# A GLA and stick-breaking decoder step: the attention mask moved into the scan, parts stored by pair and span, stores issued by ScalarE

## The reference, cut to what matters

```
proj = rmsnorm(x) @ w                     # q, k, v, gate rows
z = q . k / 8 + bias[head]                # every query t, key s
lneg = where(s < t, log_sigmoid(-z), 0)
suffix = reverse_cumsum(lneg) - lneg      # sum over s < j < t
w = where(s < t, exp(log_sigmoid(z) + suffix), 0)
o = w @ v                                 # strictly causal: s < t only
```

## Time and profile before

| | us |
|---|---|
| median of 3 runs | 3365.58 (3365.28 to 3365.92) |
| profiled execution, its own time | 3368.11 |
| its span | 3366.5 |
| mean granted TensorE clock | 0.969 of 2.4 GHz |
| PE busy | 3155.3 (94%) |
| DVE busy | 1661.5 (49%) |
| ACT busy | 1399.5 (42%) |
| POOL busy | 889.0 (26%) |

### The profile page before, as it was taken

The page is one execution under the profiler, slowest core; times in us unless marked ns, Lnnn a source line. Parts: engine busy times, 40 slices in busy tenths (PEclk is TensorE's granted clock), DMA queues, the critical chain, the costliest instruction groups (busy, mean ns, idle before and its releaser), DMA issues. The chain is left out here.

```text
span 3366.5 us, 49760 instructions
## 1 busy us (share of the span) xinstructions
PE 3155.3 (94%) x17836; PEld 2474.9 (74%) x17836; DVE 1661.5 (49%) x1967; ACT 1399.5 (42%) x2332; POOL 889.0 (26%) x936
## 2 busy tenths in 40 slices
PE   6999999799799799999999499999999999799998
PEld 6999999556588699999999355555555555466665
DVE  5111122387544411222222388998899897443442
ACT  5111111265311211112211278888888787344442
POOL 0000000254111000000000266776677675100000
PEclk8999999799899899999999699999999999899999
DMA  4122111455255421444431555343433410999995
GB/s 152 62 71 76 69 57 58 159 187 182 103 183 178 147 76 51 176 170 147 165 101 57 137 151 142 79 123 107 119 88 103 123 36 16 354 325 374 366 339 210
DMA packets 257393, 489.74 MB, mean 145 GB/s; under 512 B 27133, under 2 KB 142562, under 8 KB 245922
## 3 DMA queue, kind: packets, MB, share of 16 engines
q1 hardware_dynamic: 232450, 350.61, 32.3%
q0 software_dynamic: 24752, 136.63, 11.3%
HBM read 329.58 MB, written 157.59 MB: 145 GB/s over the span
## 5 line engine op out<-in xcount | busy, mean ns | idle before, releaser
L1736 POOL TENSOR_TENSOR att_w<-att_w,att_rest 128x1023 f32<-128x1023 f32 (+7 forms) x384 | 615.4, 1606 | 303.0 <-DVE att_rest L1703 289.9
L470 PE MATMUL projb_acc<-projb_x_hi,projb_w_hi 128*128 128x416 f32 x1280 | 451.0, 352 | 16.5 <-DVE projb_w_lo L452 16.5
L470 PE MATMUL projb_acc<-projb_x_hi,projb_w_lo 128*128 128x416 f32 x1280 | 449.2, 351 | 0.0
L470 PE MATMUL projb_acc<-projb_x_lo,projb_w_hi 128*128 128x416 f32 x1280 | 448.9, 351 | 0.0
L1564 PEld LDWEIGHTS att_wT_acc<-const_ident,att_w 128*128 128x128 f32 x2176 | 236.9, 142 | 210.2 <-issue 152.9
L1653 ACT ACTIVATE att_rest<-att_z,att_bias 128x1024 f32<-128x1024 f32 (+7 forms) x384 | 333.3, 868 | 85.4 <-PE att_z L1610 55.5
L1703 DVE TENSOR_TENSOR_SCAN att_rest<-att_rest,att_zero 128x128 f32<-128x128 f32 (+7 forms) x256 | 355.0, 1402 | 23.2 <-ACT att_rest L1653 23.1
L292 PE MATMUL proja_acc<-proja_x_hi,proja_w_hi 128*128 128x416 f32 x1000 | 353.7, 354 | 0.8 <-DVE proja_x_lo L265 0.7
L292 PE MATMUL proja_acc<-proja_x_hi,proja_w_lo 128*128 128x416 f32 x1000 | 351.8, 352 | 0.0
L292 PE MATMUL proja_acc<-proja_x_lo,proja_w_hi 128*128 128x416 f32 x1000 | 350.0, 350 | 0.0
L1564 PE MATMUL att_wT_acc<-const_ident,att_w 128*128 128x128 f32 x2176 | 314.9, 281 | 31.2 <-ACT att_k_tok L1668 14.8
(11 more groups left out here) (256 smaller groups left out, 4910.4 us busy)
## 6 DMA issues: line engine op xcount, KB each, us to landing
smp_k_pages<-in_cache_k SPq DMA_DIRECT2D x128, 512.0 KB, 7.2
smp_v_pages<-in_cache_v SPq DMA_DIRECT2D x128, 512.0 KB, 7.2
proj_b<-projb_out POOLq DMA_DIRECT2D x32, 1040.0 KB, 4.4
proj_a<-proja_out POOLq DMA_DIRECT2D x24, 1040.0 KB, 4.5
kq_hi<-early_area POOLq DMA_DIRECT2D x16, 1024.0 KB, 6.0
kq_lo<-early_area POOLq DMA_DIRECT2D x16, 1024.0 KB, 8.9
att_q_hi<-kq_hi SPq DMA_DIRECT2D x60, 256.0 KB, 4.1
att_q_lo<-kq_lo SPq DMA_DIRECT2D x60, 256.0 KB, 5.1
```

The costliest lines, as they stand in the source:

```text
L470: mm = pe.matmul(acc[:, q, 0:size], w[:, b, k, :], x[:, k, at:at + size], start=(k == 0 and w is w_hi and x is x_hi), stop=(k == KD - 1 an ...
L1736: pool.tensor_tensor(these, these, passed[:, 1:size], ALU.mult).then_inc(w_made, 1)
```

## The change

- The masking matmul goes. `begin` is an identity, transposed into the last 128 columns of a PSUM bank in bfloat16 with zeros before them; the scan of a step that is not carried reads it backwards as data1 and starts from 0, so the running product is 0 until the diagonal adds its 1. Carried steps broadcast its first zero. GpSimd's multiply takes one column more.
- The parts go to DRAM as `k_parts` and `q_parts`, by pair, span, part: ACT issues four stores of half of the partitions for a block (2 KB runs) in place of two of all. A pair's keys come back in one load (L1461 to L1468 before), a span's queries in four as before, each row now 4 KB in one run. The first pieces of pair 0 are no longer cut at the first tile.
- ACT issues the stores of both projections and waits for them at the end; GpSimd has no work there.
- The turns of pair 0 move to beats 6, 8, 10, 12; the first value step of a group waits for its own turn, not for all.
- GLA's gate weights of the second head are asked for ahead of the six output weights. ACT loads the sqrt table at the head of the first and third stage.

```diff
 normalise_project, scalar:
+            act.preload_act_table_set("sqrt_and_others")
             act.wait_ge(eps_set, 1)
...
+                if gate:
+                    act.wait_ge(gate_made, (n - first_gate) * n_spans + n_spans)
+                else:
+                    act.wait_ge(copied, n * n_spans + n_spans)
+                act.wait_ge(gain_in, 32)
+                act.dma_start(dst[ds(n * P, width), :], out[0:width, b, :]).then_inc(stored[b], 16)
 project, scalar (the gpsimd blocks of both are deleted):
                         if q == 0 and from_tile(no, 1):
-                            act.wait_ge(parts_stored, no * 32)
+                            act.wait_ge(parts_stored, no * 64)
...
+                act.dma_start(dst[ds(jb * P + row, P), :], out[:, b, :]).then_inc(stored[b], 16)
+                if kind == "parts":
+                    act.wait_ge(high_made, no * n_spans + n_spans)
+                    act.wait_ge(low_made, no * n_spans + n_spans)
+                    to = parts[j].rearrange("a u e p h n -> e h p (a u) n")
+                    for part, made in enumerate((high, low)):
+                        for h in range(2):
+                            act.dma_start(to[part, h, :, ds(jb * NCH, NCH), :],
+                                          made(0, SEQ).bitcast(F32)[h * HD:(h + 1) * HD, :].rearrange("p (u n) -> p u n", n=BANK)
+                                          ).then_inc(parts_stored, 16)
 gla, sync:
-            early.load(sp)
             sp.wait_ge(logit_cp, 5)
             gate_weights(1)
+            early.load(sp)
 out_project, scalar:
+            act.preload_act_table_set("sqrt_and_others")
 attention_schedule:
-            put(7 + m if pair == 0 else 40 * (pair - 1) + LAG + 1 + 2 * m, ("turn", pair, m))
+            put(6 + 2 * m if pair == 0 else 40 * (pair - 1) + LAG + 1 + 2 * m, ("turn", pair, m))
 prompt_attention, sync:
             def load_k(pair):
-                for u in range(NCH):
-                    load_k_span(pair, u, 0, 4, in_k[pair % 2])
+                sp.dma_start(k2[:, pair % 2, :, :, :], k_parts[pair].rearrange("u e p h n -> (e p) u (h n)")
+                             ).then_inc(in_k[pair % 2], 16)
+            def load_first_k(u):
+                sp.dma_start(k2[:, 0, u, :, :], k_parts[0, u].rearrange("e p h n -> (e p) (h n)")).then_inc(in_first_k[u], 16)
             def load_q(pair, g):
                 for part, dst in enumerate((q_hi, q_lo)):
                     for half in range(2):
-                        sp.dma_start(dst[half * HD:(half + 1) * HD, g, :, :],
-                                     head_rows(part, q_parts + pair * P)[:, :, g * BANK:(g + 1) * BANK]
-                                     ).then_inc(in_q[g], 16)
+                        sp.dma_start(dst[half * HD:(half + 1) * HD, g, :, :], q_parts[pair, g, part]).then_inc(in_q[g], 16)
...
-            load_first_q(0, 0, 1)
-            load_first_k(0, 0, 1)
+            load_q(0, 0)
+            load_first_k(0)
             sp.dma_start(bias[:, 0, :], b_sb.unsqueeze(0).broadcast_to([P, NH])).then_inc(bias_in, 16)
-            load_first_q(2, 0, 1)
-            load_first_k(2, 0, 1)
-            load_first_q(0, 1, 4)
-            load_first_k(0, 1, 4)
-            load_first_q(2, 1, 4)
-            load_first_k(2, 1, 4)
+            load_q(0, 2)
+            load_first_k(2)
 tensor:
-                if j == 4 * g + 3:
-                    pe.wait_ge(copied[1], turn_end[pair])
+                if j % 4 == 3:
+                    pe.wait_ge(copied[1], ring_no["turn", pair, j // 4] + 1)
...
-                if not carried:
-                    pe.matmul(z_ps[:, n % 2, size - P:size], c.ident_bf[:, :], c.diag_mask[:, :], start=True,
-                              stop=False, skip_group_check=True)
...
+            pe.wait_ge(begin_cleared, 1)
+            pe.transpose(begin[:, 1024 - P:1024], c.ident_bf[:, :], c.ident_bf[:, :]).then_inc(begin_made, 1)
 vector:
+                        dve.tensor_tensor_scan(passing, passing, begin[:, 0:1].broadcast_to([P, size]),
+                                               carry_of(t, h), ALU.mult, ALU.add).then_inc(scanned, 1)
+                    else:
+                        dve.tensor_tensor_scan(passing, passing, begin[:, 1024 - size:1024][:, ::-1],
+                                               rest[:, n % n_rest, 1024:1025], ALU.mult, ALU.add).then_inc(scanned, 1)
```

More of the change, by code:

```diff
@@ L324, in _ @@
             over_blocks(pe, step)
[L326 to L338, removed]
 def project(nc, c, name, xnT, jobs, parts, early):
@@ L495, in _ @@
             over_blocks(pe, step)
[L497 to L501, removed]
-                    pool.wait_ge(gate_made, no * n_spans + n_spans)
-                else:
-                    pool.wait_ge(copied, n * n_spans + n_spans)
-                pool.wait_ge(gain_in, 16 * len(jobs))
-                _, _, _, dst, row = jobs[j]
-                pool.dma_start(dst[ds(jb * P + row, P), :], out[:, b, :]).then_inc(stored[b], 16)
-                if kind == "parts":
-                    pool.wait_ge(low_made, no * n_spans + n_spans)
-                    pool.dma_start(parts[0][ds(no * P, P), :], high(0, SEQ).bitcast(F32)).then_inc(parts_stored, 16)
-                    pool.dma_start(parts[1][ds(no * P, P), :], low(0, SEQ).bitcast(F32)).then_inc(parts_stored, 16)
-            over_blocks(pool, step)
-            pool.wait_ge(stored[0], 16 * (n_blocks // 2))
-            pool.wait_ge(stored[1], 16 * (n_blocks // 2))
-            pool.wait_ge(parts_stored, 32 * n_parts)
 def gla(nc, c, projT, w_alpha2, b_alpha, state_in, state_prompt, state_sample, o_out, sums, early):
@@ L1383, in prompt_attention @@
     k_rows, v_rows, g_rows = 0, D, 3 * D
-    k_parts, q_parts = 0, D
+    k_parts, q_parts = parts
     order = attention_schedule()
@@ L1456, in _ @@
         def _(sp):
-            def head_rows(part, at):
-                return parts[part][at:at + P, :].rearrange("(h p) n -> p h n", p=HD)
-            def load_k_span(pair, u, lo, hi, sem):
-                cols = slice(u * BANK + lo * P, u * BANK + hi * P)
-                for half in range(2):
-                    sp.dma_start(k2[half * HD:(half + 1) * HD, pair % 2, :, cols],
-                                 head_rows(0 if u % 2 == half else 1, k_parts + pair * P)[:, :, cols]).then_inc(sem, 16)
-            def load_k(pair):
-                for u in range(NCH):
-                    load_k_span(pair, u, 0, 4, in_k[pair % 2])
-            def load_first_q(g, lo, hi):
-                for part, dst in enumerate((q_hi, q_lo)):
-                    for half in range(2):
-                        sp.dma_start(dst[half * HD:(half + 1) * HD, g, :, lo * P:hi * P],
-                                     head_rows(part, q_parts)[:, :, g * BANK + lo * P:g * BANK + hi * P]
-                                     ).then_inc(in_first_q[g, lo], 16)
+            def load_k(pair):
+                sp.dma_start(k2[:, pair % 2, :, :, :], k_parts[pair].rearrange("u e p h n -> (e p) u (h n)")
+                             ).then_inc(in_k[pair % 2], 16)
+            def load_first_k(u):
+                sp.dma_start(k2[:, 0, u, :, :], k_parts[0, u].rearrange("e p h n -> (e p) (h n)")).then_inc(in_first_k[u], 16)
             def load_q(pair, g):
@@ L1728, in _ @@
                     n, size = z_no[(kind, pair, *x)], hi - lo
-                    passed = rest[:, n % n_rest, 1024 - size:1024]
+                    passed = rest[:, n % n_rest, 1024 - size:1025]
+                    n_passed = size - 1 if carried else size
                     pool.wait_ge(sig_made, n + 1)
@@ L1734, in _ @@
                     pool.wait_ge(scanned, n + 1)
-                    these = weight(pair, phase, h, t, 0, size - 1)
-                    pool.tensor_tensor(these, these, passed[:, 1:size], ALU.mult).then_inc(w_made, 1)
+                    these = weight(pair, phase, h, t, 0, n_passed)
+                    pool.tensor_tensor(these, these, passed[:, 1:n_passed + 1], ALU.mult).then_inc(w_made, 1)
                     if lo:
```

71 lines of the change are left out of this document (36 added, 35 removed).

## The result

The changed kernel takes 3325.49 us in the median of 4 runs (3320.42 to 3331.59), the kernel before 3365.75 beside it (3365.28 to 3370.68, 4 runs): ratio 0.9878, interval 0.9859 to 0.9897. Forecast were 3315, between 3298 and 3340. A second set of runs gave 3326.91 against 3366.66, ratio 0.988 (0.9865 to 0.9895).

What follows compares the result with a forecast made beforehand. PE was taken to set the pace of steady attention, DVE close behind, with waiting in pair 0. The terms summed to -50.6 us from 3368.1 profiled: 3317.5 profiled, 3315 for the median, range 3298 to 3340.

Steps and rivals of the forecast that it cites:

- Turns: Pair 0 of attention: turns two beats apart cover the landing of k's store that ACT's copy awaits; -12 us.
- rival B: Pair 0: turn stalls stay, as stores of k go last on SP's queue behind a larger key load; 3327, chance 0.10.
- Seams: Stage ends and start: ACT's stores remove GpSimd's drains, -4.5 and -2.2 us; a table preload hides at the start, -2.8.
- GLA: Second head's logits: gate weights asked for first land before PE needs them, ending its stall and slower stretch; -5.5 us.
- Masks: Attention beats: without masking matmuls PE saves 2.4 us a pair, and the scan's streamed row costs nothing; -18 us.
- Start of attention: Head of attention: first step about 2 us later, but next pieces come whole and the eighth step is earlier; -6 us.
- rival C: Stage seams: they give nothing, since the time is that of landing, whoever issues the store; 3322, chance 0.09.
- Middle of the projections: Projections: ACT issues the stores in time and PE does not wait for their landings; 0 us.
- preload of the third stage: Start of the third stage: ACT's table preload stands where DVE is busy anyway; +0.4 us.
- Rivals A and D: Attention: A, masks yield nothing, 3333, chance 0.12; D, the scan is slowed by its streamed data1, 3460, chance 0.05.

Runs made afterwards that it cites:

- run 2: The kernel before with only the mask moved into the scan: 3351.97 us, ratio 0.9955.
- run 4: The changed kernel with the store of k issued first at every turn, ahead of the loads: 3320.99 us.
- run 3: The changed kernel with the turns of pair 0 back at beats 7, 8, 9, 10: 3326.12 us against 3326.91 in the same set.
- runs 9 to 12: The changed kernel with loads of pair 0 early: 3321.45; pair 1's keys late: 3323.35; both: 3315.67; both, k stores first, pair 1's turns later: 3311.40 us.
- run 6: The changed kernel with GLA's gate weights of the second head asked for behind the six output weights again: 3331.91 us.
- the kernel with both moves: The changed kernel with 2.5 MB of pair 0's loads issued first and pair 1's keys at the end of pair 0's third phase: 3315.67 us.

## Why the prediction was right, and the step that failed

The mechanism was right in every term but one, the turns. That the median came out at 3325 is what rival B gave (3327), and B's sign is there as well: waits above 5 us at the copy of k (5.3 and 6.5), and pair 0 at 128.8 for the 122 of the forecast. The terms that gave more than forecast (seams, start and GLA, 4 us) make up for masks and start of attention, which gave 3.7 less; that they cancel is luck.

- **Masks** (-18): about -16; alone, in run 2, 14.7 by the medians. Steady pairs 2.0 us each where 2.4 was taken, of 3.7 that the masks' matmuls held. The mechanism and the scan's free input were right. By phases (from the two timelines) the eight masks of the fourth phase bring 0.9 us, their full 0.12 each; the eight of the third 0.6; the sixteen of the first 0.7 of 1.9; the last phase, without masks and with DVE busy throughout, loses 0.2. At 0.12 each that is some 18 masks of the 32 of a pair, where the prediction counted 25; most of the difference is the first phase, in which PE is busy 22.1 of 23.6 us now.
- **Turns** (-12): this step failed. The prediction took the landing (about 8 us) for a fixed time and asked only whether the next turns leave room for it, and it put that room at 12 us. The landing was itself made of what the DMA engines had been given before: SP's issues from 1888 to 1903 hold 2.5 MB of keys and queries of pair 0, raw k and v, a first MB of the next pair's queries and its 2 MB of keys, and a store takes 9 to 16 us. The room was 4.4 and 6.8 us, in part since SP issues the store behind its turn's loads (with the store first, in run 4, it was 8.3 and 7.6). The kernel before showed full engines already: 242 GB/s at a share of 1.10, read there as a rate of halves and not as a queue. More room is worth nothing by run 3. The second phase of pair 0, where the waits lie, takes 39.8 and 42.0 us in the two profiles of the changed kernel, 41.7 before. So the term is 0 to 2 where 12 stood: that is the 10 us between 3315 and 3325. It is rival B, by another mechanism: not one 2 MB load ahead of one store, but all of pair 0's transfers after an idle stretch (runs 9 to 12).
- **Start of attention** (-6): the first step comes 2.9 us later behind the first load, and the first phase is 7.9 shorter (23.2 for 31.2), of which 0.7 by the masks: -4.3 for -6. No run has the new loads alone, but the runs leave little else: with the new mask and the old loads the first phase takes 32.1 us (run 2), with the new loads and the old beats of the turns 23.7 (run 3). Over the profiles with the new loads the first step comes 1.9 to 4.8 us later.
- **Seams** (-4.5, -2.2, -2.8): -6.1, -3.5, -2.9, each on the good side, the first two a little beyond their bounds of -6 and -2.8; rival C falls. The first load comes 1.6 us sooner than forecast, since ACT's landing, 4.1 us, is no longer than GpSimd's 4.4.
- **GLA** (-5.5): -6.5 in the profile, beyond the bound of -6, -5.2 by the means of run 6.
- **Middle of the projections** (0) and **preload of the third stage** (+0.4): right, -0.2 and +0.6; no run shows the second apart.
- Rivals A and D fall on the scan at 1403 ns and the pair at 114.7.

## What to carry to other kernels

A wait for a landing says who is last, not what is slow: before moving the waiting step, look at the share of the DMA engines around it, and for an idle stretch ahead of the burst into which loads whose buffers are free can be moved. Moving the consumer, adding a buffer and reordering the queue gave 0, 0 and 6 us here; moving 4.5 MB of loads gave 10 to 11. A mask can go into an operand that an engine reads anyway, which cost nothing here (scans at 1403 ns for 1402), but its price on the busiest engine is the period of a beat with and without it, times the beats which that engine binds.

## What had not been expected of the hardware

- GpSimd's drain after the second projection is 5.28 us in the kernel before and 2.67 with GpSimd's stores in the new layout; ACT's end shows none at that place. Why it differs wasn't tried.
- Full DMA engines are not one rate. In the kernel with both moves, the loads that move from 1877 to 1883 us are, by the order of their issue and landing, raw k and v and keys, mostly over all partitions, and from 1884 to 1891 queries in halves of the partitions. The share is 1.05 in both, and they move 400 and 230 GB/s:

```profile
1877.00:1883.00 6.00, 3.89 (x12) 2.93 (x12) 2.73 (x5) 3.51 (x11) 2.29 (x6) 0.50 1.05 400
1884.00:1891.00 7.00, 5.14 (x12) 2.59 (x12) 4.98 (x6) 5.58 (x11) 5.20 (x10) 0.50 1.05 230
```

- Identical work in GLA and the last pair ran at a clock of 0.93 or 1.00 from execution to execution, worth 1.6 us in a stretch of 24 and some 5 us a run.
